# Group normalization of a recurrence's output: from pair by pair to two passes with one variance tile, and constants made beside the first norm

## What is computed

```
mean = jnp.mean(y, axis=-1, keepdims=True)          # over the 64 channels of a head
var = jnp.mean(jnp.square(y - mean), axis=-1, keepdims=True)
yn = ((y - mean) * lax.rsqrt(var + LNX_EPS)).reshape(B, T, D_RWKV) * lw['lnx_w'] + lw['lnx_b']
out = (yn + bonus.reshape(B, T, D_RWKV)) * g
```

## Time and profile before

| | |
|---|---|
| time, median of 3 runs | 3871.38 us (3859.22 to 3874.24) |
| the profiled execution, own time | 3879.54 us |
| its span in the trace | 3877.9 us |
| busy: PE, DVE, ACT, POOL | 3492.0, 1434.2, 1013.2, 476.6 us |
| mean granted clock of TensorE | 0.927 |
| DMA | 423.90 MB, mean 109 GB/s |

### The profile page before, as it was taken

How to read it: one execution, slowest core, us unless ns; L and a number is a source line. 1 busy time by engine, 2 the same in 40 slices (tenths; PEclk the granted TensorE clock), 3 DMA queues, 4 the chain that set the end, 5 groups by cost and what they waited for, 6 DMA issues and landing times. The chain is left out here.

```text
span 3877.9 us, 68987 instructions
## 1 busy us (share of the span) xinstructions
PE 3492.0 (90%) x29790; PEld 3160.8 (82%) x29790; DVE 1434.2 (37%) x1811; ACT 1013.2 (26%) x1408; POOL 476.6 (12%) x531
## 2 busy tenths in 40 slices
PE   5999999569964999869977989999999999999998
PEld 5999999248853777644334989999999999999997
DVE  3222221553245666325533223333333333233334
ACT  4111110433222665313421222121221221212112
POOL 1000000353422333400000000000000000000000
PEclk8999998569876999778988999999999999999999
DMA  5433321565515454342343332332332333333332
GB/s 162 118 109 110 108 82 42 162 195 130 137 43 196 174 205 152 110 136 44 73 134 119 87 76 88 88 98 88 88 98 88 98 88 90 96 88 97 89 88 99
DMA packets 506389, 423.90 MB, mean 109 GB/s; under 512 B 144613, under 2 KB 458454, under 8 KB 501518
## 3 DMA queue, kind: packets, MB, share of 16 engines
q1 hardware_dynamic: 481630, 302.76, 27.6%
q0 software_dynamic: 15392, 115.99, 8.2%
q10 hardware_dynamic: 9136, 1.72, 0.2%
HBM read 381.94 MB, written 65.76 MB: 115 GB/s over the span
## 5 line engine op out<-in xcount | busy, mean ns | idle before, releaser
L2724 DVE TENSOR_TENSOR f_w_lo<-wo_raw,f_w_hi 128x2048 fp32r<-128x2048 f32 x132 | 302.5, 2292 | 817.7 <-ACT f_w_hi L2696 817.7
L53 PE MATMUL d_ps<-hh,f_w_hi 128*128 128x260 f32 x2816 | 567.5, 283 | 12.4 <-DVE f_w_lo L2724 11.9
L57 PE MATMUL d_ps<-hh,f_w_lo 128*128 128x260 f32 x2816 | 568.0, 283 | 0.0
L55 PE MATMUL d_ps<-hl,f_w_hi 128*128 128x260 f32 x2816 | 567.1, 283 | 0.0
L2696 ACT CAST f_w_hi<-wo_raw 128x2048 fp32r<-128x2048 f32 x132 | 252.0, 1909 | 997.2 <-DMA wo_raw<-in_w_gate 394.4
L53 PEld LDWEIGHTS d_ps<-hh,f_w_hi 128*128 128x128 f32 x2816 | 434.8, 189 | 13.3 <-DVE f_w_lo L2724 12.6
L57 PEld LDWEIGHTS d_ps<-hh,f_w_lo 128*128 128x128 f32 x2816 | 434.6, 189 | 0.0
L55 PEld LDWEIGHTS d_ps<-hl,f_w_hi 128*128 128x128 f32 x2816 | 433.4, 188 | 0.0
L53 PE MATMUL d_ps<-f_hid_hi,f_w_hi 128*128 128x260 f32 x1408 | 283.8, 283 | 1.1 <-DVE xt L2748 1.0
L57 PE MATMUL d_ps<-f_hid_hi,f_w_lo 128*128 128x260 f32 x1408 | 283.4, 283 | 0.0
L55 PE MATMUL d_ps<-f_hid_lo,f_w_hi 128*128 128x260 f32 x1408 | 282.4, 282 | 0.0
(11 more groups left out here) (447 smaller groups left out, 5946.1 us busy)
## 6 DMA issues: line engine op xcount, KB each, us to landing
p_w<-in_w_in SPq DMA_DIRECT2D x46, 1024.0 KB, 5.6
wo_raw<-in_w_gate SPq DMA_DIRECT2D x44, 1024.0 KB, 5.7
wo_raw<-in_w_up SPq DMA_DIRECT2D x44, 1024.0 KB, 5.7
wo_raw<-in_w_down SPq DMA_DIRECT2D x44, 1024.0 KB, 5.1
wo_raw<-in_w_o SPq DMA_DIRECT2D x16, 1024.0 KB, 6.0
sel_d<-in_cache_slc_kv SPq DMA_DIRECT2D x364, 32.0 KB, 2.1
rk_chunks<-r_outb POOLq DMA_DIRECT2D x8, 1280.0 KB, 6.2
s_cur<-rk_chunks SPq DMA_DIRECT2D x8, 1280.0 KB, 7.5
```

What stands on the lines that cost most here:

```text
L53: pe.matmul(out[j], w_hi, x_hi[j], start=start, stop=False)
L55: pe.matmul(out[j], w_hi, x_lo[j], start=False, stop=False)
L57: last = pe.matmul(out[j], w_lo, x_hi[j], start=False, stop=stop)
L2724: dve.tensor_tensor(w_lo[:, s, :], w_raw[:, s, :], w_hi[:, s, :].bitcast(F32), ALU.subtract).then_inc(lo_done, 1)
```

## The change

Two things, and a third that goes with them.

1. `stage_constants` is no block any more. Its instructions are `make_constants`, at the head of POOL's list in `stage_norm`, in front of `keep_x`. PE waits for the first two of them (the identity) before its first transpose.
2. `stage_rwkv_post` runs in two passes. First pass, by pair: mean on PE, one centring instruction on DVE over all 520 columns, in place in `y_t`; square on ACT into a tile that holds all pairs; a variance matmul with a weight matrix of 16 columns (`gather16`, shifted by two for each pair), which adds each pair's two rows to one PSUM tile of 16 partitions, one row a head. Then once, in two halves: mean plus epsilon, root, reciprocal, on 16 partitions. Second pass, by pair: PE spreads two of the 16 rows over 128 partitions (`spread`), DVE multiplies by weight and reciprocal in one instruction, adds the bonus, to which ACT has added the shift, and multiplies by the gate, all in place. POOL makes the two weight matrices at the stage's start.
3. Semaphores are retired, cleared and released at more places: by SP in the chunk stage and the compress stage, by POOL in the FFN.

The diff, without the removed lines of the output stage and the body of the constants, which is unchanged:

```diff
@@ -105,7 +105,7 @@
         stored_prompt = new_sem(nc, g, "n_stored_prompt")
         stored_sample = new_sem(nc, g, "n_stored_sample")
         x_stored = [new_sem(nc, g, f"n_x_stored{i}") for i in range(2)]
-        chain = new_sem(nc, g, "n_chain")
+        chain, made = new_sem(nc, g, "n_chain"), new_sem(nc, g, "n_made")
         tiles = [(g.x_prompt[r:r + n, :], r, n) for r, n in ROW_TILES[:4]]
         tiles += [(g.x_sample, SEQ, NB), (g.shift, TC, NB)]
         NT = len(tiles)
@@ -196,6 +196,7 @@
             @block.tensor
             def _(pe):
+                pe.wait_ge(made, 2)
                 for i, (_s, _c, n) in enumerate(tiles):
                     if i < 5:
                         pe.wait_ge(loaded[i % 3], 16 * (i // 3 + 1))
@@ -217,6 +218,8 @@
             @block.gpsimd
             def _(pool):
+                make_constants(pool, g, made)
+
                 def keep_x(i):
                     r, n = ROW_TILES[i]
                     pool.wait_ge(x_kept, 4 * i + 4)
@@ -875,6 +878,8 @@
                     if c >= 1:
                         load_sample(c - 1)
                         copy_new_rows(sp, g, c - 1)
+                    if c == 1:
+                        clear_old(sp, g)
                 load_sample(CH - 1)
                 copy_new_rows(sp, g, CH - 1)
@@ -1159,21 +1164,33 @@
 def stage_rwkv_post(nc, g):
...
     HC = TC // 2
+    H = 2 * NPAIR
     with ExitStack() as ctx:
...
+        sq = ctx.enter_context(nc.sbuf_tensor("e_sq", [P, NPAIR, TC], F32))
+        rs = ctx.enter_context(nc.sbuf_tensor("e_rs", [H, 3, TC], F32))
         vec = ctx.enter_context(nc.sbuf_tensor("e_vec", [P, 2, NPAIR], F32))
+        gather16 = ctx.enter_context(nc.sbuf_tensor("e_gather", [P, 2 * H], F32))
+        spread = ctx.enter_context(nc.sbuf_tensor("e_spread", [H, D_R], F32))
         ps = ctx.enter_context(nc.psum_tensor("e_ps", [P, 8, 512], F32))
...
+        made, vec_in, mean_done, yc_ready = (new_sem(nc, g, "e_" + n) for n in ("made", "vec_in", "mean_done", "yc_ready"))
         sq_ready, var_done, ve_ready, root_ready = (new_sem(nc, g, "e_" + n) for n in
                                                     ("sq_ready", "var_done", "ve_ready", "root_ready"))
...
+        bonus_ready, rec_ready, spread_done, spread_read = (new_sem(nc, g, "e_" + n) for n in (
+            "bonus_ready", "rec_ready", "spread_done", "spread_read"))
+        chain, out_ready, stored = new_sem(nc, g, "e_chain"), new_sem(nc, g, "e_out_ready"), new_sem(nc, g, "e_stored")
+        var = ps[0:H, 4:6, 0:HC]
+
+        def both(t):
+            return t.rearrange("p (h t) -> p h t", h=2)
+
+        def mean_bank(q):
+            return ps[:, 2 * (q % 2):2 * (q % 2) + 2, 0:HC]
+
+        def spread_bank(q):
+            lo = (0, 2, 6)[q % 3]
+            return ps[:, lo:lo + 2, 0:HC]
+
         with nc.Block() as block:
             @block.sync
             def _(sp):
@@ -1183,79 +1200,96 @@
                 clear_old(sp, g)
                 for q in range(NPAIR):
                     sp.wait_ge(out_ready, q + 1)
...
+                    sp.dma_start(g.mix_t[q * P:(q + 1) * P, :], g.y_t[:, q, :]).then_inc(stored, 16)
+                sp.wait_ge(stored, 16 * NPAIR)
+
+            @block.gpsimd
+            def _(pool):
+                step = Chain(pool, made)
+                step(pool.memset(gather16[:], 0.0))
+                step(pool.tensor_copy(gather16[:, H - 2:H], g.blk64[:].rearrange("p (a c) -> p a c", a=2)[:, :, 0]))
+                step(pool.memset(spread[:], 1.0))
+                v = spread[:].rearrange("p (n w) -> p n w", w=C)
+                for sign in (-1, 1):
+                    step(pool.affine_select(out=v, in_=v, compare_op=ALU.is_ge, fill=0.0, base=0, pattern=[[sign, H], [0, C]],
+                                            channel_multiplier=-sign))
             @block.tensor
             def _(pe):
                 def mean(q):
                     if q >= 2:
...
+                        pe.wait_ge(yc_ready, q - 1)
                     for h in range(2):
...
+                        last = pe.matmul(mean_bank(q)[:, h, :], g.blk64[:], g.y_t[:, q, h * HC:(h + 1) * HC],
                                          start=True, stop=True)
                     last.then_inc(mean_done, 1)
+
+                def variance(q):
+                    pe.wait_ge(sq_ready, q + 1)
+                    for h in range(2):
+                        last = pe.matmul(var[:, h, :], gather16[:, H - 2 - 2 * q:2 * H - 2 - 2 * q], sq[:, q, h * HC:(h + 1) * HC],
+                                         start=(q == 0), stop=(q == NPAIR - 1))
+                    last.then_inc(var_done, 1)
+
                 mean(0)
+                mean(1)
+                pe.wait_ge(made, 2)
                 for q in range(NPAIR):
...
+                    if q + 2 < NPAIR:
+                        mean(q + 2)
+                    variance(q)
+                pe.wait_ge(made, 5)
+                for q in range(NPAIR):
+                    if q >= 3:
+                        pe.wait_ge(spread_read, q - 2)
                     for h in range(2):
...
+                        if q == 0:
+                            pe.wait_ge(rec_ready, h + 1)
+                        last = pe.matmul(spread_bank(q)[:, h, :], spread[:, q * P:(q + 1) * P], rs[:, 2, h * HC:(h + 1) * HC],
                                          start=True, stop=True)
...
+                    last.then_inc(spread_done, 1)
             @block.scalar
             def _(act):
+                act.wait_ge(vec_in, 32)
                 for q in range(NPAIR):
...
+                    act.wait_ge(yc_ready, q + 1)
+                    act.activation(sq[:, q, :], g.y_t[:, q, :], ACT.Square).then_inc(sq_ready, 1)
+                for h in range(2):
+                    act.wait_ge(ve_ready, h + 1)
+                    w = slice(h * HC, (h + 1) * HC)
+                    act.activation(rs[:, 1, w], rs[:, 0, w], ACT.Sqrt).then_inc(root_ready, 1)
+                for q in range(NPAIR):
+                    act.activation(g.bonus_t[:, q, :], g.bonus_t[:, q, :], ACT.Identity, bias=vec[:, 1, q:q + 1]).then_inc(bonus_ready, 1)
             @block.vector
             def _(dve):
                 step = Chain(dve, chain)
...
+                for q in range(NPAIR):
                     dve.wait_ge(mean_done, q + 1)
...
+                    y = both(g.y_t[:, q, :])
+                    dve.scalar_tensor_tensor(out=y, in0=mean_bank(q), scalar=-1.0 / C, in1=y, op0=ALU.mult,
+                                             op1=ALU.add).then_inc(yc_ready, 1)
+                dve.wait_ge(var_done, NPAIR)
+                for h in range(2):
+                    w = slice(h * HC, (h + 1) * HC)
+                    dve.tensor_scalar(rs[:, 0, w], var[:, h, :], 1.0 / C, 64e-5, ALU.mult, ALU.add).then_inc(ve_ready, 1)
+                for h in range(2):
+                    w = slice(h * HC, (h + 1) * HC)
+                    dve.wait_ge(root_ready, h + 1)
+                    dve.reciprocal(rs[:, 2, w], rs[:, 1, w]).then_inc(rec_ready, 1)
                 dve.wait_ge(vec_in, 32)
...
+                dve.wait_ge(yc_ready, NPAIR)
+                dve.wait_ge(sq_ready, NPAIR)
+                for q in range(NPAIR):
+                    y = both(g.y_t[:, q, :])
+                    dve.wait_ge(spread_done, q + 1)
+                    dve.scalar_tensor_tensor(out=y, in0=y, scalar=vec[:, 0, q:q + 1], in1=spread_bank(q), op0=ALU.mult,
+                                             op1=ALU.mult).then_inc(spread_read, 1)
+                    dve.wait_ge(spread_read, q + 1)
+                    dve.wait_ge(bonus_ready, q + 1)
+                    step(dve.tensor_tensor(g.y_t[:, q, :], g.y_t[:, q, :], g.bonus_t[:, q, :], ALU.add))
+                    dve.tensor_tensor(g.y_t[:, q, :], g.y_t[:, q, :], g.gate_t[:, q, :], ALU.mult).then_inc(out_ready, 1)
 def stage_compress(nc, g):
@@ -2639,6 +2674,7 @@
             @block.gpsimd
             def _(pool):
+                clear_old(pool, g)
                 pool.wait_ge(rstd_ready, 1)
                 with pool.Fori(0, PARTS) as i:
...
-def stage_constants(nc, g):
...
+def make_constants(pool, g, made):
+    step = Chain(pool, made)
...
+    step(pool.memset(g.ident[:], 0.0))
+    band(g.ident[:], [[-1, P]], 1, 0, ALU.not_equal, 1.0)
...
@@ -2973,7 +3003,9 @@
         g.chunk_decay = sb("chunk_decay", [P, NPAIR, SEQ // C])
         g.v_samp = sb("v_samp", [P, NPAIR, NB])
         stage_rwkv_prep(nc, g)
+        retire_sems(g)
         stage_rwkv_chunks(nc, g)
+        release_old(nc, g)
         retire_sems(g)
         stage_rwkv_post(nc, g)
         release_old(nc, g)
@@ -3005,7 +3039,6 @@
     g.xt_d = nc.dram_tensor("xt_d", [P, KT, TC], F32, kind="Internal").ap()
     with ExitStack() as ctx:
         constants(nc, g, ctx)
-        stage_constants(nc, g)
         with ExitStack() as c2:
             g.xh = c2.enter_context(nc.sbuf_tensor("xh", [P, KT, TA], F32R))
@@ -3017,9 +3050,9 @@
```

(75 more changed lines are left out.)

72 lines of the change are left out of this document (removed).

## The result

The changed kernel takes 3828.4 us, the median of 4 runs (3826.18 to 3831.37), against 3867.52 of the kernel before (3859.22 to 3874.24): 0.9903 of its time, interval [0.9888, 0.9918]. The forecast was 3828.4 us in a range of 3812 to 3846. That the two medians agree to the hundredth is luck: the forecast starts from 3871.4, and further runs of the kernel before had medians near 3864, so the gain itself is 35 to 39 us where 43 was forecast.

What follows compares the result with a forecast made beforehand. PE was busy 90% of the span, but the start was serial behind GpSimd's constants and the output stage was DVE's. Saving 15.0 + 28.0 = 43.0 us from 3871.4 gave 3828.4 us, range 3812 to 3846.

Steps and rivals of the forecast that it cites:

- Start: Kernel start, constants made beside the first norm: SP's first load 15.4 us earlier, counted as 15.0 us saved.
- The 0.4 us taken off for mutual holds: First norm: 0.4 us deducted from the 15.4 us gain for engines holding each other up.
- The slack of 2.3 us for `keep_x(0)`: First norm: its transfer, queued behind the constants, lands at 22.1; ScalarE wants the buffer at 24.4.
- constants and norm hold each other up: Rival, first norm: GpSimd and DVE contend, giving between 3831 and 3841 us, from rows 3835; chance 0.12.
- Pass one: Output stage, mean and variance of all pairs: PE sets it, 17.4 us, ends 15.3 and 29.2.
- The clock's rise: Output stage, first pass: PE goes from half to full clock 4.6 us after its first matmul.
- the distance of records at full clock: Output stage, first pass: 54 PE records at 0.234 us each, after 10 at 0.45.
- half clock in pass one: Rival, output stage: PE stays at half clock, 29.2 us instead of 17.4, total 3840.2 us; chance 0.12.
- Between and pass two: Output stage: root, reciprocals and first spreading product 5.4 us; then DVE's 2.2 us a pair, 17.8 us.
- Tail: Output stage's end, from last result to the next stage's beginning: 2.6 us, as before.
- Given back: Later stages: expected to move rigidly; rival, 24 us or more given back, about 3855 us, chance 0.07.
- Clears: Semaphore clearing in chunk, compress and FFN stages: costs nothing; up to 6.5 us if SP's chunk-stage cover were gone.

Runs made afterwards that it cites:

- e1: Kernel before with only the constants moved to the head of GpSimd's list in the first norm: 3852.8 us, ratio 0.9972.
- e2: Kernel before with the two-pass output stage and the semaphores' new places, constants still in their own block: 3841.6 us, ratio 0.9952.
- f1: Changed kernel with the second half of the triangular masks made after the second store in GpSimd's list: 3821.74 us, 0.9899 of the kernel before.
- g0_after: The changed kernel run once more, unchanged: 3827.15 us, 0.9911 of the kernel before.
- f2: Changed kernel with a third pair of PSUM banks for the means, issued three pairs ahead: 3826.39 us, 0.9909 of the kernel before.
- e3_sems: Kernel before with only the retiring, clearing and releasing of semaphores at the new places: 3864.9 us, ratio 0.9998.
- after: The changed kernel itself, as first measured and profiled: 3828.4 us, 0.9903 of the kernel before.
- f3: Changed kernel with the gate multiplied in during the first pass, leaving DVE two instructions in the second: 3826.58 us, 0.9901 of the kernel before.
- f4: Changed kernel with late masks, third pair of mean banks and gate multiplied in during the first pass: 3837.16 us, 0.9922 of the kernel before.
- g1: Changed kernel with late masks and gate multiplied in during the first pass, two pairs of mean banks: 3826.81 us, 0.9901 of the kernel before.

## Why the prediction was right, and where its terms were off

**The cause is the one forecast.** Each of the two places shrank by itself (e1, e2), in the stages where it was looked for. The constants came off the front because nothing else ran there; the output stage shrank because DVE's work in it fell from 59.99 to 26.36 us, until PE set its first pass.

**Start: 14.05 instead of 15.0.** The 15.4 are exact. The 0.4 us taken off for mutual holds was the mis-sized term, and it is 1.34. The slack of 2.3 us for `keep_x(0)` was reckoned without a hold, and the rival used it up with one hold of 2.35; two `L151` fall inside the constants, they cost 3.8, and ScalarE waits 1.76. In f1, without this queue, the norm is 42.80 again. A norm longer than 42.7 was one of the forecast's own signs of being wrong, and it came. The rival "constants and norm hold each other up" is thus true as a mechanism and small: 0.9 us beyond the 0.4 of the sum, below the least that it was priced at (2.6). The Trainium skill, "GPSIMD Engine Reference", section "Key points", names contention between GpSimd and DVE instructions with two SBUF inputs; the trace agrees. In these rows only GpSimd pays (0.45 to 2.49 us, 0.21 to 1.97), not DVE (2.35 in all of them), and in each DVE's instruction had begun first. The kernel before has the other order in the recurrence's first stage:

```profile
776.15 1.42 POOL L558 TENSOR_TENSOR r_cum<-r_cum,r_sw 128x512 f32<-128x512 f32 x1 [1.47 <-DVE r_cum L743]
...
776.48 1.65 DVE L747 SCALAR_TENSOR_TENSOR r_kf<-r_kf,r_k_all 128x520 f32<-128x520 f32 x1
...
778.17 0.76 DVE L752 SCALAR_TENSOR_TENSOR r_rkk<-r_xr,r_vec,r_kf 128x520 f32<-128x520 f32 x1
```

There GpSimd began first, and DVE's `L747` takes 0.89 us longer than `L752`, the same operation on as many columns with nothing of GpSimd beside it. In these rows the second to begin is the one that ends late; no run turned the order round for one and the same pair.

**Pass one: 18.75 and 17.6 for a forecast of 17.4.** PE sets it, as forecast. `g0_after` gives the second value; its whole pass as one window, and the one in which the clock rises:

```profile
1094.00:1096.00 2.00, 2.00 (x9) 1.21 (x8) 1.23 (x2) 1.09 (x2) 0.61 (x1) 0.92 0.00 0
...
1090.86:1108.43 17.57, 17.57 (x64) 9.39 (x64) 5.59 (x8) 6.38 (x9) 3.49 (x5) 0.90 0.07 1
```

PE's records fill 17.57 of 17.57 us. The clock's rise is no constant: 3.5 us after the first matmul here (0.92 of 2 us), 5.9 in the profiled execution, 4.6 in the forecast. At 0.22 us a record that runs at the half clock instead of the full one, these are 8, 13 and 10 records, -0.4 and +0.7 us against the forecast. The term that was mis-sized in both is the distance of records at full clock: 0.257, where 0.234 was forecast, because the earlier trace rows is one run of records with like matrices, and here four of the mean alternate with four of the variance. Where the last 12 variance records follow each other they are (2.81 - 0.38) / 11 = 0.22 apart; four means take 1.07 to the start of the next group, four variances 0.98. With the slightly shorter run at the end set against it, that is 0.6 to 0.7 us over the pass. f2 excludes a wait for a buffer; what in the alternation costs 0.1 to 0.2 us a group isn't settled. The rival "half clock in pass one" didn't happen; the clock fell in pass two, where the sum had counted PE at half clock already.

**Between and pass two.** 5.76 instead of 5.4: the surplus is in the first spreading product, multiplied in 1.37 us after PE's second start (1113.50 and 1114.87), where 0.95 and a hand-over were summed. And 17.16 instead of 17.8: the product with the spread tile begins 0.09 us before the end of the product in front of it (1117.01 and 1117.10), so a pair takes 2.14 and not 2.2. Tail 2.48, forecast 2.6. The stage is 44.15 us, and 43.0 in `g0_after`, for a forecast of 43.2. GpSimd's masks were over 3.8 us after the stage's start, 17.8 us before they were wanted. ScalarE's wait for `vec_in` stood in front of nothing: its first Square began 0.1 us after its input.

**Given back: 1.8 us, unforeseen.** In all eight profiled executions with the new output stage the unchanged output projection takes 211.2 to 211.9 us, in all four with the old one 209.2 to 209.9. The forecast put this at nothing: the stages in between were to move rigidly. The rows of `mix_raw` there, in `e3_sems` and then in `e2_post` (waits for this tile's transfer, total and times):

```profile
  DMA mix_raw<-mix_t: 5.7, 4
```

```profile
  DMA mix_raw<-mix_t: 7.1, 4
```

ScalarE waits for the last loads of `mix_t`, the rows that the new stage's and the attention's stores write, 1.4 us longer in sum (5.0 to 5.7 us in the four executions with the old stage, 7.0 to 7.8 in the eight with the new one). In the code only the stage's stores to `mix_t` differ for them, in their times and their source tile. Why the loads land later is open; no kernel tried it. Beside it the stage in front of the output projection (the picked attention) took 93.3 to 95.0 us in eight of the twelve profiled executions and 97.3 to 97.7 in four, all with the new output stage (after, f3, f4, g1), while e2, f1, f2 and g0 have the lower value. The changed kernel itself has both, 97.3 in its first profiled execution and 95.0 in `g0_after`, so at least that much is the execution; whether the change makes the longer one likelier is open. The 1.8 us are a given-back loss by their kind, and far below the 24 us of that rival.

**Clears: nothing**, by e3 (0.9998) and the row above.

**The sum.** 14.05 + 27.1 - 1.8 = 39.3 us by the trace; by the ratio, 0.0097 x 3867, 37.5 (32 to 43). The forecast said 43.0 from a median that was 4 us above the next one measured. Its error in the gain (3.7) and in the base (3.9) cancelled, which is luck.

## What to carry to other kernels

A reciprocal on DVE costs by columns: sixteen rows once instead of 128 rows eight times took 24 us of DVE's time out of a stage that was DVE's, and after it the first pass was PE's, the second DVE's with 0.4 us a pair to spare; look up the bound of each pass before shortening anything more. Constants can be made beside the first work, if no engine's store or load stands behind them in the queue. And cut two profiles by stage before explaining their difference: 20 of 53.6 us here were the clock of one execution, and a second run of unchanged code showed 17 of them.

## What the runs showed of the hardware

- The chunk stage, with the same work in all, took 265.2 to 285.8 us in twelve profiled executions, at a granted clock of 0.98 to 0.90 (265.2 to 268.9 in nine of them). That spread is half of what the whole change brings. The rise at the start of the output stage came 3.5 us after the first matmul in one execution and 5.9 in another of the same code.
- A select of GpSimd on 64 partitions that takes 0.2 us alone took 1.97, and two took 2.49, beside a DVE instruction with two inputs from SBUF; the one ends at 19.31, DVE's at 19.23. DVE took 2.35 us with and without. Where GpSimd had begun first, a DVE instruction with two inputs from SBUF took 1.65 us in place of 0.76.
- PE's records with weights of 16 rows filled 13.4 us without a gap, 0.44 us each, and the clock stayed at 1.2 GHz throughout, in the changed kernel and in `f3_gate_first`. Records of 128 rows were followed by a rise to 2.4 GHz within 5.9 us in the same stage. What makes the difference was not tried, and the two differ in more than the rows.
- Half the columns of a reciprocal take half the time, on 16 partitions too: 3.40 us for two of 16x260, 3.40 for one of 128x520 in the earlier trace rows.
